# One store where there were two and four: expert outputs, query and key weights, and the final sum in a two-layer YOCO step

## The chip, the cores and the metric

The kernel runs on one core of one Trainium2 chip. The metric is device time in microseconds (us) of one execution, from start to end; lower is better. TensorE, VectorE, ScalarE, GpSimd and SyncE are called PE, DVE, ACT, POOL and SP in the profile. 16 DMA engines move the data; the queues that SP, ACT and POOL fill are q1, q10 and q0 there.

## What is computed

One inference step of a two-layer decoder trunk in float32, width 1024, for 512 prompt tokens and 32 sample tokens (8 sequences of 4). Layer 0 is an HGRN2 recurrence, layer 1 is differential attention over shared keys and values, which for the sample tokens reach back over 2048 cached positions in pages. Behind each stands a mixture of 16 experts, of which each token uses two:

```python
def hier_moe(h, w_group, w_sub, w_gate, w_up, w_down):
    ...
    eid = gidx[..., None] * MOE_EPG + idx                      # two experts of one group
    gates = jnp.einsum('btke,btk->bte', jax.nn.one_hot(eid, MOE_EXPERTS, dtype=F32), w2)
    hid = jax.nn.silu(jnp.einsum('btd,edf->btef', h, w_gate)) * jnp.einsum('btd,edf->btef', h, w_up)
    hid = hid * gates.astype(h.dtype)[..., None]
    return jnp.einsum('btef,efd->btd', hid, w_down)            # D = 1024, f = 256

for l in range(DEPTH):                                         # DEPTH = 2
    h = h + mixer(rmsnorm(h, norm_mix_w[l]))                   # HGRN2, then differential attention
    h = h + hier_moe(rmsnorm(h, norm_ffn_w[l]), ...)
    if l == 0:                                                 # keys and values of layer 1
        kv = rmsnorm(h, kv_norm_w) @ w_kv
y = rmsnorm(h, final_norm_w)
```

The queries of layer 1 are `rmsnorm(h, norm_mix_w[1]) @ b_w_q`.

## The kernel before

The 544 tokens stand as five tiles: four of 128 prompt rows (t = 0 to 3) and one of 32 sample rows (t = 4). The residual stream `h` stays in SBUF. The work is one program with blocks for the stages; in a block each engine runs its own list of instructions in the order in which the code writes them, and semaphores tie the engines together. Nothing reorders them, so a change of order in the code is a change of order on the engine.

**The expert loop** (class Experts, from line 1519), the same for both layers. A token's row has been sent to a slot of its expert in DRAM (`slots_x`); an expert has 96 slots (CAP), 64 wide and 32 narrow. SP loads each expert's 96 rows, its gate and up weights (two loads of 1 MB) and its down weights (1 MB) into a ring of five experts' slots, all in one queue. For expert e PE computes gate and up (L1739, L1744), turns the rows of expert e + 1 (L1716), computes down for expert e - 1 (L1764, L1768) and turns the hidden rows of e (L1752, L1753). ACT takes the SiLU (L1613, L1614), DVE multiplies with the up half (L1662) and moves the turned hidden rows out (L1669, L1671). The 64 wide rows of the result stand in bank 5 as 128 partitions x 512: columns 0 to 511 of the rows on partitions 0 to 63, columns 512 to 1023 on partitions 64 to 127. The 32 narrow rows stand in bank 6 as four such quarters of 256 columns. ACT copies the wide ones to SBUF (`YW`, L1620), DVE the narrow ones (`YN`, L1678). ACT then issues the stores to `slots_y` in DRAM: two DMAs for the wide rows (L1623) and four for the narrow ones (L1597), one for each half or quarter; each adds 16 to `y_out` of that buffer when it has landed, and `STORES` = 6 is what the waits reckon with. The narrow rows of the last expert are stored by SP. `slots_y` has a row of 1024 floats for each slot.

If more tokens want an expert than it has slots, a branch behind the loop takes the rest (`more > 0`). Each engine reads the number of these blocks from SBUF (`more_blocks`, L1549) and jumps over the branch where it is zero.

**Behind the loop.** `finish` (L1790) runs on PE: it waits until all stores have landed, then adds to `finished`. POOL waits for that and issues ten indirect gathers, two for each token tile (a token's two experts), from `slots_y`.

- Layer 0: the gathers are those of L1811, the sample tile first (`SAMPLE_FIRST`). DVE adds them, times the gates, to `h` (L1824); `add(dve, i)` adds both rows of the i-th tile of that order. Then the norm for layer 1 is made tile by tile: squares on ACT (L2177), root (L2179), scaling on DVE (L2190), turned on PE (L2205), and copied into `xT` by DVE and ACT (L2218, `out_first`; L2225, `out_second`). PE's sample queries (L412) follow on the sample tile.
- Class Projections prepares the query and key weights meanwhile. Each of the four halves (q0, q1, k0, k1, 128 x 4096) is multiplied with the norm's weight row. ACT does q0 and k0 with eight activations each (L2272, x16 in the profile), DVE q1 and k1 with one instruction each of 128 x 4096 (L2281). The table `PROJECT_SCALED` holds which unit of PE's projections waits for how many of these. A few loads of pages and of weights for this stage stand in SP's queue behind the last experts'.
- Layer 1 (class SumOnBanks, from L1864; `last_block`, L1945): the sum is made on the banks. PE enters `h` of a tile by a multiplication with the identity (`residual`, L1904, two matmuls per tile), then adds the gathered rows with diagonal matrices of the gates (`add`, L1913). Tile t uses banks 2t and 2t + 1. Tiles 0 and 1 are entered before PE's `finish`, tiles 2 and 3 behind it, all of them behind the branch. ACT squares the banks (L1924), DVE scales them with the final norm (L1941), SP stores the result.

**At the start** ACT issues twelve small loads (class Setup, L199 to L203): six of 8 rows x 128 (L199, weight vectors of 1024) and six of a single row (L200, L201, L203: two norm weights and four lambda vectors).

## Time and profile before

| | |
|---|---|
| three runs | 1472.49, 1474.75, 1483.41 us, median 1474.75 us |
| the profiled execution | 1480.49 us, its span 1478.7 us |
| mean granted TensorE clock | 0.935 |
| PE busy | 1305.8 us, 88% of the span |
| DVE busy | 723.8 us, 49% |
| ACT busy | 411.2 us, 28% |
| POOL busy | 176.3 us, 12% |
| moved by DMA | 348.15 MB in 133,902 packets |
| expert loop of layer 0 | about 487 to 657 us |
| expert loop of layer 1 | about 1274 to 1441 us |

All times are microseconds from the start of the span in that one execution. A row of the timeline has start, duration, engine, line of the kernel, operation, output<-input by the program's names, shapes, count, and in brackets how long the engine sat idle before it and what ended that. "ACTq" and "SPq" are the sequencers that issue DMAs. PE counts a float32 matmul as several passes, so 8 matmuls stand as x16. The granted clock is a share of full speed. A share of DMA is the mean busy share of the 16 engines.

### The profile page before, as it was taken

The page shows a single profiled execution, that of the slowest core. Times are in us where ns is not written, and L with a number is a line of the kernel's source. Part 1 is how long each engine was busy: PE and PEld are TensorE (multiplying, and loading weights), DVE is VectorE, ACT ScalarE, POOL GpSimd, SP SyncE. Part 2 cuts the span into 40 slices and gives each one's busy share as a digit, 9 for nine tenths or more (in the row PEclk, how much of TensorE's full clock was granted, in tenths as well). Part 3 has the DMA queues.
Part 4 walks back from the last instruction along what each step waited for, and adds up shares of the span by engine and source line. Part 5 has one row for each costly group of instructions (what it writes and reads, how often), then busy time and mean ns, then how long its engine had stood idle before and what let it go on. Part 6 is the DMA issues. An engine that isn't in the chain of part 4 may idle for free. (4 is left out here: it accounts for less than half of the span.)

```text
span 1478.7 us, 29953 instructions
## 1 busy us (share of the span) xinstructions
PE 1305.8 (88%) x11855; PEld 770.3 (52%) x11855; DVE 723.8 (49%) x1881; ACT 411.2 (28%) x1098; POOL 176.3 (12%) x247
## 2 busy tenths in 40 slices
PE   6999999998799998976999989868778699899897
PEld 3445565565356654534555545445454355755543
DVE  4435777676655311137343544377874465411123
ACT  3024445453210211133213121134455211121112
POOL 2002223322011000013021100100100001000002
PEclk9999999999898899997999999988988799799998
DMA  6150435223804899994465899799999631899935
GB/s 231 58 149 6 134 107 182 74 77 131 288 36 170 308 367 356 320 329 169 150 220 218 329 347 361 302 405 374 408 378 343 219 140 52 339 379 343 338 94 189
DMA packets 133902, 348.15 MB, mean 235 GB/s; under 512 B 22603, under 2 KB 52478, under 8 KB 125566
## 3 DMA queue, kind: packets, MB, share of 16 engines
q1 hardware_dynamic: 115378, 311.53, 59.0%
q10 hardware_dynamic: 13388, 16.82, 3.4%
q0 software_dynamic: 4992, 17.83, 3.3%
q8 instruction: 97, 1.59, 0.4%
q14 instruction: 47, 0.39, 0.1%
HBM read 302.61 MB, written 43.52 MB: 234 GB/s over the span
## 5 line engine op out<-in xcount | busy, mean ns | idle before, releaser
L409 PE MATMUL bank<-wring,xT 128*128 128x512 f32 x448 | 200.4, 602 | 0.0
L409 PEld LDWEIGHTS bank<-wring,xT 128*128 128x128 f32 x448 | 84.1, 192 | 100.6 <-issue 100.5
L1440 PE MATMUL bank<-wring,xT 128*128 128x512 f32 x256 | 120.2, 623 | 2.0 <-DVE xT L1360 2.0
L883 PE MATMUL bank<-xT,wring 128*128 128x512 f32 x256 | 113.7, 602 | 3.9 <-DVE hgrn_g L707 3.9
L2803 DVE STREAM_TRANSPOSE attn_k_pages<-attn_k_pages 128x1024 f32<-128x1024 f32 x64 | 77.6, 1232 | 40.4 <-DMA attn_k_pages<-cache_k 39.9
L883 PEld LDWEIGHTS bank<-xT,wring 128*128 128x128 f32 x256 | 48.7, 192 | 65.3 <-issue 59.8
L1440 PEld LDWEIGHTS bank<-wring,xT 128*128 128x128 f32 x256 | 49.6, 200 | 60.1 <-issue 59.9
L2803 DVE STREAM_TRANSPOSE wring<-wring 128x1024 f32<-128x1024 f32 x44 | 52.5, 1222 | 49.2 <-DMA wring<-cache_k 49.2
L785 DVE COPY_PREDICATED gla_att<-level_masks,bank 128x512 f32<-128x512 int32 x48 | 35.1, 731 | 72.1 <-PE bank L903 72.0
L2316 PE MATMUL bank<-xT,wring 128*128 128x512 f32 x128 | 56.9, 597 | 0.0
L903 PE MATMUL bank<-gla_qe,gla_ke 128*128 128x128 f32 x384 | 49.9, 285 | 0.0
L1662 DVE TENSOR_TENSOR hgrn_g<-hgrn_g,bank 128x128 f32<-128x128 f32 x32 | 7.8, 284 | 84.7 <-ACT hgrn_g L1613 84.7
L1662 DVE TENSOR_TENSOR attn_qo<-attn_qo,bank 128x128 f32<-128x128 f32 x32 | 7.8, 284 | 82.6 <-ACT attn_qo L1613 82.6
L903 PEld LDWEIGHTS bank<-gla_qe,gla_ke 128*128 128x128 f32 x384 | 46.4, 197 | 3.1 <-DVE gla_att L785 2.6
L569 ACT ACTIVATE gla_diff<-gla_diff 128x512 f32<-128x512 f32 (+1 forms) x48 | 30.6, 638 | 57.5 <-DVE gla_diff L750 48.4
L1620 ACT ACTIVATE moe_norm_w<-bank 128x512 f32<-128x512 f32 x32 | 19.1, 597 | 81.5 <-PE bank L1768 81.5
L2926 ACT ACTIVATE attn_shared<-attn_shared,pa_stat 128x128 f32<-128x128 f32 (+2 forms) x64 | 35.2, 556 | 17.3 <-DVE pa_stat L2786 17.3
L844 POOL TENSOR_TENSOR gla_ke<-gla_k,gla_diff 128x256 f32<-128x256 f32 x40 | 32.1, 802 | 53.3 <-ACT gla_diff L569 53.3
L2610 POOL TENSOR_SCALAR attn_shared<-attn_shared 128x512 f32<-128x512 f32 x8 | 11.9, 1491 | 222.4 <-DVE pa_stat L2786 144.3
L2316 PEld LDWEIGHTS bank<-xT,wring 128*128 128x128 f32 x128 | 23.7, 190 | 27.8 <-issue 27.8
L2680 PE MATMUL bank<-attn_k_pages,sa_q 128*32 128x128 f32 x1024 | 31.1, 273 | 7.4 <-DVE sa_red L2812 7.4
L840 POOL TENSOR_TENSOR gla_ke<-gla_k,gla_diff 128x544 f32<-128x544 f32 x8 | 10.9, 1362 | 212.5 <-ACT gla_diff L562 212.5
(460 smaller groups left out, 2403.2 us busy)
## 6 DMA issues: line engine op xcount, KB each, us to landing
attn_k_pages<-cache_k SPq DMA_DIRECT2D x64, 512.0 KB, 7.6
wring<-cache_v SPq DMA_DIRECT2D x56, 512.0 KB, 7.8
wring<-cache_k SPq DMA_DIRECT2D x44, 512.0 KB, 7.0
moe_wd<-moe_w_down SPq DMA_DIRECT2D x20, 1024.0 KB, 13.6
attn_shared<-cache_v SPq DMA_DIRECT2D x40, 512.0 KB, 5.7
wring<-moe_w_gate SPq DMA_DIRECT2D x18, 1024.0 KB, 11.2
wring<-moe_w_up SPq DMA_DIRECT2D x18, 1024.0 KB, 14.8
wring<-a_w_in SPq DMA_DIRECT2D x16, 1024.0 KB, 10.5
```

Source lines behind the costliest of these rows:

```text
L409: last = nc.tensor.matmul(bank[:, :], xT[:, c, cols(t)], w[:, c, :], start=(c == 0), stop=(c == DC - 1))
L569: nc.scalar.activation(diff[i % 2][:, 0:w], diff[i % 2][:, 0:w], ACT.Exp).then_inc(exp_ready, 1)
L785: nc.vector.copy_predicated(A[:, :, :], bcast(k.levelmask[:, i, :].bitcast(I32), 1, [P, PT, P]), k.ps[3 + i % 2][:, :].rearrange("p (c n) ...
L844: nc.gpsimd.tensor_tensor(blocks(KE[j][:, :], size)[:, :, lo], blocks(kk[:, 0:SEQ], size)[:, :, lo], blocks(diff[j % 2][:, 0:SEQ], size)[: ...
L883: last = nc.tensor.matmul(bank[:, :], lhsT, k.xT[:, c, 0:SEQ], start=(c == 0), stop=(c == DC - 1))
L903: last = nc.tensor.matmul(k.ps[3 + i % 2][:, part], KE[i][:, part], QE[i][:, part], start=True, stop=True)
L1440: last = nc.tensor.matmul(bank[:, :], k.xT[:, c, cols(t)], w[:, c, :], start=(c == 0), stop=(c == DC - 1))
L1620: nc.scalar.activation(self.YW[u][:, :], k.ps[5][:, :], ACT.Copy).then_inc(self.y_a, 1)
L2316: last = nc.tensor.matmul(bank[:, :], w[:, c, (t % 4) * P:(t % 4 + 1) * P], k.xT[:, c, 0:SEQ], start=(c == 0), stop=(c == DC - 1))
L2680: last = nc.tensor.matmul(out.rearrange("p (r x) -> p r x", r=GROUP), Q[b % 2][:, h, i, :], keys.K[s][:, :, at:at + QUAD], start=(i == 0), ...
L2803: nc.vector.transpose(page, page).then_inc(keys_turned, 1)
L2926: last = nc.scalar.activation(part, part, ACT.Exp, bias=s[:, x, 2 + c:3 + c], accum_out=s[:, x, 4 + c:5 + c])
```

## The change

1. **Two stores for each expert in place of six.** The wide rows go out in one DMA, the narrow ones in one. The destination is written as [2, 64 rows, 512 columns] and [4, 32 rows, 256 columns], the source is the whole tile of 128 partitions. `STORES` becomes 2.
2. **Scaling of weights on DVE.** `gates_ready` becomes a general hook `beside`, called behind the hidden rows of the last two experts. In layer 0 it now runs `weights_by_vector(0)` (k1 whole) behind expert 14's and `weights_by_vector(1)` (the first half of q1) behind expert 15's; the second half of q1 follows behind the branch.
3. **Scaling on ACT.** q0 whole as before; then the root of the first tile, the first half of k0, the copies of the first tile, the second half of k0, the root of the second tile. `PROJECT_SCALED` and the wait of the sample queries follow suit.
4. **Adds of the second tile on DVE** are split: the first choice before `out_first(0)`, the second behind it.
5. **The end of layer 1.** Tiles use banks (0, 1), (4, 5), (6, 7), (2, 3). PE enters three tiles ahead of the branch: tile 0 behind the last down matmuls, tile 1 when ACT has copied bank 5, tile 2 when DVE has copied bank 6. Inside the branch they are closed first and entered again at its end. Tile 3 follows behind the branch. `finish` is run by DVE there instead of PE; in layer 0 it stays on PE. Inside the branch DVE waits for the stores.

```diff
@@ Experts
-NB, STORES = 2, 6
+NB, STORES = 2, 2
         eng.wait_ge(self.y_v, j + 1)
-        for n in range(4):
-            eng.dma_start(self.slot_rows(row, WIDE, NARROW)[:, n * 2 * P:(n + 1) * 2 * P], self.YN[u][n * NARROW:(n + 1) * NARROW, :])\
-                .then_inc(self.y_out[u], 16)
+        eng.dma_start(self.slot_rows(row, WIDE, NARROW).rearrange("r (n c) -> n r c", n=4), self.YN[u][:, :])\
+            .then_inc(self.y_out[u], 16)
...
-            for n in range(2):
-                act.dma_start(self.slot_rows(row, 0, WIDE)[:, n * HB:(n + 1) * HB], self.YW[u][n * WIDE:(n + 1) * WIDE, :])\
-                    .then_inc(y_out[u], 16)
+            act.dma_start(self.slot_rows(row, 0, WIDE).rearrange("r (n c) -> n r c", n=2), self.YW[u][:, :])\
+                .then_inc(y_out[u], 16)
...
-            if e >= E - 2 and gates_ready is not None:
-                gates_ready(dve, e - (E - 2))
+            if e >= E - 2 and beside is not None:
+                beside(dve, e - (E - 2))
...
+            if last_layer:
+                dve.wait_ge(self.y_out[0], 16 * STORES * (loads_before(NB, 0) + MORE))
...
         pe.wait_ge(routing.blocks_ready, 1)
+        if on_free_banks is not None:
+            on_free_banks(0)
+            pe.wait_ge(self.y_a, E)
+            on_free_banks(1)
+            pe.wait_ge(self.y_v, E)
+            on_free_banks(2)
         more = self.more_blocks(pe)
         with pe.If(more > 0):
+            if on_free_banks is not None:
+                for t in range(3):
+                    on_free_banks(t, start=False, stop=True)
...
+            if on_free_banks is not None:
+                for t in range(3):
+                    on_free_banks(t)
@@ SumOnBanks, last_block
     def banks(self, t):
-        return [self.k.ps[2 * (t % PT) + i] for i in range(2)]
+        first = (0, 4, 6, 2)[t % PT]
+        return [self.k.ps[first + i] for i in range(2)]
...
-            ffn.experts.vector(dve, total.diagonal)
+            ffn.experts.vector(dve, total.diagonal, True)
+            ffn.experts.finish(dve)
...
-            ffn.experts.tensor(pe)
             pe.wait_ge(ffn.mix.added, 2 * NT)
-            for t in range(2):
-                total.residual(pe, t)
-            ffn.experts.finish(pe)
-            for t in range(2, PT):
-                total.residual(pe, t)
+            ffn.experts.tensor(pe, lambda t, **flags: total.residual(pe, t, **flags))
+            total.residual(pe, 3)
@@ Projections
-        for landed, kind, row in ((k.weights_landed(self.first + 1), "q", 1), ((self.k1_in, 32), "k", 2)):
-            dve.wait_ge(*landed)
-            tile = self.W[kind, 1][:, :, :]
+        landed, kind, row, c = (((self.k1_in, 32), "k", 2, slice(0, DC)),
+                                (k.weights_landed(self.first + 1), "q", 1, slice(0, DC // 2)),
+                                (k.weights_landed(self.first + 1), "q", 1, slice(DC // 2, DC)))[n]
+        dve.wait_ge(*landed)
+        tile = self.W[kind, 1][:, c, :]
...
-        pe.wait_ge((self.scaled_a, self.scaled_v)[i], 1)
+        pe.wait_ge(*((self.scaled_a, 1), (self.scaled_v, 3))[i])
...
-        self.weights_by_vector(dve)
+        self.weights_by_vector(dve, 2)
         add(dve, 0)
         turn_page(0, 0)
         norm.scale(dve, ch, 0)
-        add(dve, 1)
+        add(dve, 1, (0,))
         norm.out_first(dve, 0)
+        add(dve, 1, (1,))
...
-        self.weights_by_act(act)
+        queries_0, keys_0, half = (0, "q", 1), (2, "k", 2), DC // 2
+        self.weights_by_act(act, queries_0, range(DC))
         norm.load_table(act)
         norm.root(act, 0)
+        self.weights_by_act(act, keys_0, range(half))
         norm.out_second(act, 0)
+        self.weights_by_act(act, keys_0, range(half, DC))
         norm.root(act, 1)
-PROJECT_SCALED = {0: ("act", 2), 1: ("dve", 2), 14: ("pool", 1), V_SAMPLE: ("pool", 2)}
+PROJECT_SCALED = {0: ("act", 3), 1: ("dve", 1), 14: ("pool", 1), V_SAMPLE: ("pool", 2)}
...
-                ffn.vector(dve)
+                ffn.vector(dve, proj.weights_by_vector)
```

ACT, the stores of expert 0 of layer 0 and what stands ahead of them, before. `moe_norm_w` holds the wide rows, `hgrn_g` the narrow ones (and what L1606 and L1614 write), `slots_y` is in DRAM:

```order
L1613 ACTIVATE hgrn_g<-bank 128x128
L1614 ACTIVATE hgrn_g<-bank 128x128
L1606 ACTIVATE hgrn_g<-bank 128x384
L1620 ACTIVATE moe_norm_w<-bank 128x512
L1623 DMA slots_y<-moe_norm_w 64x512 x2
L1597 DMA slots_y<-hgrn_g 32x256 x4
```

And now:

```order
L1612 ACTIVATE hgrn_g<-bank 128x128
L1613 ACTIVATE hgrn_g<-bank 128x128
L1605 ACTIVATE hgrn_g<-bank 128x384
L1619 ACTIVATE moe_norm_w<-bank 128x512
L1621 DMA slots_y<-moe_norm_w 2x64x512
L1596 DMA slots_y<-hgrn_g 4x32x256
```

Six DMAs have become two, with an outer count of 2 and of 4; the activations are the same.

DVE, before, from the end of layer 0's loop (behind the branch) on; `wring` holds q1 and `attn_shared` k1:

```order
L2876 MEMSET sa_lam_row 128x4
L2877 COPY sa_lam_row<-row_gains 128x4
L2281 TENSOR_TENSOR wring<-wring,column_weights 128x4096
L2281 TENSOR_TENSOR attn_shared<-attn_shared,column_weights 128x4096
L1824 SCALAR_TENSOR_TENSOR h<-hgrn_v,stat,h 32x1024
L1824 SCALAR_TENSOR_TENSOR h<-hgrn_g,stat,h 32x1024
```

DVE now, from the hidden rows of expert 14 to the branch:

```order
L1669 TENSOR_REDUCE hgrn_g<-bank 128x2x32
L2293 TENSOR_TENSOR attn_shared<-attn_shared,column_weights 128x4096
L1660 TENSOR_TENSOR hgrn_g<-hgrn_g,bank 128x128 x2
L1676 COPY hgrn_g<-bank 128x256
L1667 COPY hgrn_g<-bank 128x2x64
L1669 TENSOR_REDUCE hgrn_g<-bank 128x2x32
L2293 TENSOR_TENSOR wring<-wring,column_weights 128x2048
L1676 COPY hgrn_g<-bank 128x256
L1549 TENSOR_LOAD slots_and_blocks
```

The keys' scaling stands before the multiplications of expert 15 (L1660), half of the queries' before the last copy of narrow rows (L1676); the other half stays behind the branch, ahead of the adds.

PE, the end of layer 1's loop, before, without the branch's own rows:

```order
L1764 MATMUL bank<-moe_wd,attn_qo 64x512 x4
L1768 MATMUL bank<-moe_wd,attn_qo 32x256 x8
L1549 TENSOR_LOAD slots_and_blocks
L1549 ISA x2
L1782 COMPARE_AND_BRANCH
...
L1782 UNCONDITIONAL_BRANCH
L1904 MATMUL bank<-h,ident 128x512 x8
L1913 MATMUL bank<-attn_qo,wring 128x512 x10
```

And now:

```order
L1764 MATMUL bank<-moe_wd,attn_qo 64x512 x4
L1768 MATMUL bank<-moe_wd,attn_qo 32x256 x8
L1917 MATMUL bank<-h,ident 128x512 x6
L1549 TENSOR_LOAD slots_and_blocks
L1549 ISA x2
L1788 COMPARE_AND_BRANCH
...
L1788 UNCONDITIONAL_BRANCH
L1917 MATMUL bank<-h,ident 128x512 x2
L1926 MATMUL bank<-attn_qo,wring 128x512 x10
```

Six of the eight residual matmuls have moved ahead of the read of the number of blocks and the jump.

## Rows read from the trace of the kernel before

**Rows 1.** The page's head.

```profile
span 1478.7 us, 29953 instructions
```

**Rows 2.** Windows in both loops: us, busy of L1620 (count), clock, DMA share, GB/s.

```profile
500.00:619.60 119.60, 6.57 (x11) 0.97 1.02 354
1280.00:1392.60 112.60, 5.97 (x10) 0.98 1.00 348
```

**Rows 3.** PE's timeline, the last wait for gathered rows in each loop.

```profile
619.62 0.88 PE L1716 MATMUL bank<-ident,hgrn_g 96*128 96x96 f32 x8 [2.14 <-DMA hgrn_g<-slots_x]
...
1392.65 0.88 PE L1716 MATMUL bank<-ident,attn_qo 96*128 96x96 f32 x8 [1.90 <-DMA attn_qo<-slots_x]
```

**Rows 4.** ACT's queue from 1436 to 1441, the last two experts' stores.

```profile
1436.16 1.12 ACTq L1623 DMA_DIRECT2D slots_y<-moe_norm_w  x2
1437.33 2.02 ACTq L1597 DMA_DIRECT2D slots_y<-attn_qo  x4
...
1440.10 1.42 ACTq L1623 DMA_DIRECT2D slots_y<-moe_norm_w  x2
```

**Rows 5.** DMA from 0 to 14: packets and share; an issue, KB each.

```profile
q10 hardware_dynamic: 108, 0.03, 0.9%
...
hgrn_g<-norm_mix_w ACTq DMA_DIRECT2D x2, 4.0 KB
```

**Rows 6.** DMA from 520 to 540: packets, MB and share; an issue with landing.

```profile
q1 hardware_dynamic: 1253, 6.38, 90.9%
q10 hardware_dynamic: 704, 0.79, 11.3%
...
slots_y<-moe_norm_w ACTq DMA_DIRECT2D x4, 128.0 KB, 6.9
```

**Rows 7.** DMA from 1438 to 1438.5, then an issue from 1440 to 1440.5.

```profile
q10 hardware_dynamic: 58, 0.11, 96.9%
...
slots_y<-moe_norm_w ACTq DMA_DIRECT2D x1, 128.0 KB, 2.3
```

**Rows 8.** Timeline at the end of layer 0's loop.

```profile
648.67 0.49 DVE L1662 TENSOR_TENSOR hgrn_g<-hgrn_g,bank 128x128 f32<-128x128 f32 x2 [5.34 <-ACT hgrn_g L1613]
...
655.18 0.42 DVE L1678 COPY hgrn_g<-bank 128x256 f32<-128x256 f32 x1 [3.12 <-PE bank L1768]
...
656.65 4.42 DVE L2281 TENSOR_TENSOR wring<-wring,column_weights 128x4096 f32<-128x4096 f32 x1
658.47 9.91 ACT L2272 ACTIVATE wring<-wring,column_weights 128x512 f32<-128x512 f32 x16 [2.56 <-issue]
659.71 2.12 POOL L1811 DMA_INDIRECT hgrn_v<-slots_y,slots_and_blocks  x1 [173.64 <-PEq L1795]
...
660.99 4.42 DVE L2281 TENSOR_TENSOR attn_shared<-attn_shared,column_weights 128x4096 f32<-128x4096 f32 x1
662.14 4.01 POOL L1811 DMA_INDIRECT hgrn_g<-slots_y,slots_and_blocks  x1 [0.30 <-issue]
...
670.71 1.27 DVE L1824 SCALAR_TENSOR_TENSOR h<-hgrn_v,stat,h 32x1024 f32<-32x1024 f32 x1 [5.30 <-DMA hgrn_g<-slots_y,slots_and_blocks]
...
679.33 0.28 ACT L2225 ACTIVATE xT<-bank 128x128 f32<-128x128 f32 x1 [4.43 <-PE bank L2205]
...
680.94 6.76 PE L412 MATMUL bank<-wring,xT 128*32 128x128 f32 x192 [1.65 <-DVE xT L2218]
```

**Rows 9.** Timeline at the end of layer 1's loop; last, a gather's landing.

```profile
1439.92 2.54 SPq L1597 DMA_DIRECT2D slots_y<-attn_qo  x4
...
1442.62 9.93 PE L1904 MATMUL bank<-h,ident 128*128 128x512 f32 x16 [3.22 <-issue]
...
1443.93 0.99 POOL L1887 DMA_INDIRECT attn_qo<-slots_y,slots_and_blocks  x1 [170.79 <-PEq L1795]
...
1452.38 8.75 PE L1913 MATMUL bank<-attn_qo,wring 128*128 128x512 f32 x20
...
attn_qo<-slots_y,slots_and_blocks POOLq DMA_INDIRECT x1, 4.2
```

More of the change, by code:

```diff
@@ L1813, in gpsimd, with add @@
                     .then_inc(self.landed[i], 16)
-    def add(self, dve, i):
+    def add(self, dve, i, choices=range(TOPK)):
         k, t = self.k, SAMPLE_FIRST[i]
         dve.wait_ge(self.landed[i], 16 * TOPK)
-        for j in range(TOPK):
+        for j in choices:
             n = TOPK * i + j
@@ L1848, in scalar, with vector @@
         self.experts.scalar(act)
-    def vector(self, dve):
+    def vector(self, dve, beside=None):
         self.mix.vector(dve)
-        self.experts.vector(dve)
+        self.experts.vector(dve, beside)
     def tensor(self, pe):
@@ L1898, in diagonal, with residual @@
         last.then_inc(self.diagonals, 1)
-    def residual(self, pe, t):
+    def residual(self, pe, t, start=True, stop=False):
         k = self.k
@@ L1904, in residual @@
             self.nc.tensor.matmul(bank[0:rows(t), :], k.ident[0:rows(t), 0:rows(t)], k.h[0:rows(t), t, i * HB:(i + 1) * HB],
[L1905 removed]
+                                  start=start, stop=stop)
     def add(self, pe, t):
@@ L2263, in first_pages_in, with weights_by_act, weights_by_vector @@
             self.keys.load_k(sp, 0, r)
-    def weights_by_act(self, act):
+    def weights_by_act(self, act, which, chunks):
         k = self.k
-        for n, kind, row in ((0, "q", 1), (2, "k", 2)):
-            act.wait_ge(*k.weights_landed(self.first + n))
-            for c in range(DC):
-                part = self.W[kind, 0][:, c, :]
-                last = self.nc.scalar.activation(part, part, ACT.Copy, scale=k.cw[:, row, c:c + 1])
-            last.then_inc(self.scaled_a, 1)
-    def weights_by_vector(self, dve):
-        k = self.k
-        for landed, kind, row in ((k.weights_landed(self.first + 1), "q", 1), ((self.k1_in, 32), "k", 2)):
-            dve.wait_ge(*landed)
-            tile = self.W[kind, 1][:, :, :]
-            self.nc.vector.tensor_tensor(tile, tile, bcast(k.cw[:, row, :], 2, [P, DC, HB]), ALU.mult).then_inc(self.scaled_v, 1)
+        n, kind, row = which
+        act.wait_ge(*k.weights_landed(self.first + n))
+        for c in chunks:
+            part = self.W[kind, 0][:, c, :]
+            last = self.nc.scalar.activation(part, part, ACT.Copy, scale=k.cw[:, row, c:c + 1])
+        last.then_inc(self.scaled_a, 1)
+    def weights_by_vector(self, dve, n):
+        k = self.k
+        landed, kind, row, c = (((self.k1_in, 32), "k", 2, slice(0, DC)),
[3 more added lines that the diff above has]
+        tile = self.W[kind, 1][:, c, :]
+        self.nc.vector.tensor_tensor(tile, tile, bcast(k.cw[:, row, c], 2, [P, c.stop - c.start, HB]), ALU.mult).then_inc(self.scaled_v, 1)
     def value_weights_by_pool(self, pool, i):
```

13 lines of the change are left out of this document (6 added, 7 removed).

## The prediction

> **What bounds the kernel now.** I read the windows over the two expert loops first, then what TensorE waits for in them, then what the stores cost the DMA engines, and last the timelines at the two places where a loop ends. The span is 1478.7 us [rows 1] in a run of 1480.49 us, so 1.8 us lie around it; the median of the three runs shown is 1474.75, 5.7 below that run, and I carry differences over to the median unchanged.
>
> The reader is to see that the DMA engines are full in both expert loops: share 1.02 from 500 to 619.6 and 1.00 from 1280 to 1392.6, with 11 and 10 experts' stores in these stretches [rows 2]. TensorE is just ahead of them. It waits for the gathered rows of the next expert, 2.14 us at 619.62 and 1.90 us at 1392.65 [rows 3], each time the last such wait of its loop: up to there an expert takes as long as its loads, and behind it as long as its matmuls. A loop then ends in a chain: last copy out, stores, `finished`, the gathers by POOL, the adds. So three things can change the time: work given to the DMA engines inside the loops, the time at which the last store lands, and what stands between the gathers and the next matmul.
>
> **The stores.** Before, an expert's rows leave in six DMAs of 64 or 32 rows, issued in 1.12 and 2.02 us [rows 4]. Now there are two: one writes [2, 64 rows, 512], one [4, 32 rows, 256], from 128 partitions each. Bytes and data packets stay the same: the row of two experts says 704 packets [rows 6], and 2 x (128 + 128 data + 6 x 16) = 704, so a DMA of 64 or of 32 rows ended with a small packet on each of 16 engines. What is open is over how many engines the new ones go. The trace has a case with few rows at the start: six loads of 8 rows and six of one row are all that the queue carried, and it moved 108 packets [rows 5] (the code's lines 199 to 203 give the counts). Data are 6 x 8 + 6 x 1 = 54, so 54 small ones are left, and 6 x 8 + 6 x 1 is again 54 (with 16 each they would be 192). A load of 8 rows ran on 8 engines, one of one row on one: the outermost count sets the number of engines when it is small. Here the outermost count of the destination is 2 and 4, that of the source 128. No row shows a DMA with unlike counts. I take the smaller, since a share of the work must be a whole part of both sides: 2 engines for the wide store, 4 for the narrow one.
>
> The Trainium skill, DMA: Bandwidth & Descriptors, section "Why a DMA increments its semaphore by 16 and not by 1", says it outright: the number of engines is the largest up to 16 that divides the slowest dimension of both access patterns, so an outer dimension of 2 confines the DMA to two. The 108 and 704 packets above agree with it; by it the sum is the one below, and by a split along the source's 128 rows it would be that of the first rival.
>
> The price: the stores of two experts took 11.3% of 16 engines x 20 us = 36.2 us [rows 6], 18.1 us for one expert, or 1.13 us on each engine. Two thirds of the bytes are wide: 12.1 us, on two engines 6.0 each. The narrow 6.0 us on four are 1.5 each. If the four include the two, which I assume, as both would begin at the same end, the busiest engines carry 7.5 us in place of 1.13: +6.4 per expert (5.0 if they don't share). From above: in a quiet half microsecond 58 packets of mostly 2 KB took 96.9% of 8 us [rows 7], 0.134 us each; 64 of them are 8.6, with the narrow 1.5 that makes 10.1, +9.0. I take 6.4, since the row that it comes from lies in the full stretch where it counts.
>
> Each load of weights or rows is split evenly over 16 engines and has landed when the fullest one is done. So in the full stretches every expert's loads land 6.4 us later per store put ahead of them: 11 x 6.4 = **70 us** in layer 0 and 10 x 6.4 = **64 us** in layer 1 [rows 2]. At +9.0 it is 99 and 90, at 5.0 it is 55 and 50. ScalarE is freed of some 2 us of issuing per expert, which hides behind matmuls anyway.
>
> **Where the loops end.** Layer 1: the last two wide stores are issued at 1436.16 and 1440.10 [rows 4]. At 8.6 + 1.5 us each on the busiest engines they are worked off at 1446.3 and 1456.4, and with the 1.2 us that a store needs beyond its packets (it landed in 2.3 us, 8 x 0.134 of it moving [rows 7]) the last lands at 1457.6; the first gather began at 1443.93, so it is 13.7 late. A gather landed after 4.2 us [rows 9]: the first add can start at 1461.8, not 1452.38, +9.4. The three residual tiles are done by then, so nothing is won by moving them; and after the long wait the first adds run at the low clock, as the residuals did before: the residuals' 16 passes took 9.93 us, while the adds' took 8.75 / 20 = 0.44 each, so 2.9 us were lost to the clock [rows 9]. Together **+12 us**. That VectorE now signals in TensorE's place costs nothing against a store that lands at 1457.6: even a branch as long as TensorE's 3.22 us [rows 9] is over by 1443.2.
>
> Layer 0: the last stores are late in the same way, and loads of pages and weights stand on the same engines: **+14 us** at least. Against it stand the scalings. VectorE's two took 4.42 us each, and POOL's first two gathers took 2.12 and 4.01 us under them [rows 8], where a gather of layer 1 takes 0.99 [rows 9]; the first add began at 670.71 [rows 8]. Now the key weights go into the idle 5.34 us before 648.67 (4.42 fit, with 0.9 to spare) and half the query weights into the 3.12 us before 655.18 (2.2 fit) [rows 8]. The last 2.2 us run from 656.65 to 658.9, ahead of the gathers. The two gathers then take 2.3 us (2 x 0.99 and 0.3 between) instead of the 6.4 from 659.71 to 666.15: -4.2. One add of 1.27 us is no longer ahead of the copy that frees TensorE at 680.94: -1.3. ScalarE's first key half, 4 x 0.62 us (9.91 / 16), fits into its idle 4.43 us before 679.33; the second makes the next square 1.4 us later, which the 6.76 us of matmuls at 680.94 cover [rows 8]. If the query weights land late on the full engines, VectorE's copy of the last expert waits behind them, a few us. Sum **-5.5 us**; net for this end +8.5.
>
> **Sum.** 70 + 8.5 + 64 + 12 = 154.5 us: 1480.5 becomes 1635, and the median 1474.75 becomes **1629 us**.
>
> **Rivals.** (1) The stores keep 16 engines, because the split follows the source's 128 rows. For it speaks only that no row shows unlike counts. Then the loops lose nothing and save 64 small packets per expert, at the mean of 0.051 us (36.2 / 704) 0.2 us per expert, at most 4. `finished` comes about 1.4 us sooner at each end, as four SP stores of 2.54 us become one [rows 9]; layer 0 gains 5.5 + 1.4. In layer 1 the six moved matmuls are 12 passes, which run while TensorE would have idled 3.22 us for the branch, if its sequencer works on the branch while matmuls are queued. Then residuals end near 1446.5, the first gather lands near 1447, and the adds gain about 5; if it doesn't, the idle time and the low clock only move behind them: 0. Take 4. Together -11, with some of the packets -13: 1462 us (1458 to 1468). This is the one that ends on the other side, and the number of engines decides it: already at 8 for both stores the busiest carry 18.1 / 8 = 2.3 us, +1.1 per expert or 24 us in all, more than everything else gains.
>
> (2) Few engines, but the loads don't wait for them: if the full share is a limit of the memory and not of each engine, the two could do more while the rest idle. Against it: the share of all engines is 1.0, and the load queue and the stores add up to it (90.9% and 11.3% [rows 6]). Then only the ends count: 14 + 12 - 5.5 = +20.5, 1495 us.
>
> (3) The upper price: each 2 KB packet takes 0.134 us in the full stretches too. 99 + 90 + 20.5 = +209, 1684 us.
>
> **Chances.** Few engines with loads held up 0.77 (of it 0.12 near rival 3), rival 2 0.06, 16 engines 0.17. The likeliest gives 1629; its own range, by 5.0 and 9.0 per expert, is 1595 to 1684, and 1560 to 1700 with what I don't know of the waits between. The range that leaves out rival 1 alone and the tails is 1490 to 1700. A measurement can tell about 1% (15 us) from no change. Rival 1 lies at -0.9% and is faster by over 1% one time in four: faster 0.05, same 0.12, slower 0.83.
>
> **What would show it.** Right: packets of the ACT queue per expert fall from 352 to 262 (256 data, 2 + 4 small) and not to 288; a wide store takes 10 us and more to land instead of 2.3 in the quiet stretch; TensorE waits about 5 us before every transposed expert from the sixth or so on, for slots_x; the mean share of the 16 DMA engines in the loops falls to about 0.65; the first two gathers of layer 0 take about 1 us each. Wrong: 288 small-and-data packets, shares still at 1.0, loops as long as before. If the waits are there but shorter than 5 us, the price per packet is off; if the loops stay and only the ends move, rival 2 holds.

## The result, and the profile after

The changed kernel takes 1584.96 us (median of 4 runs, 1580.79 to 1589.07) against 1479.08 us for the kernel before in the same rounds: 1.0716 times as long, 95% interval 1.0678 to 1.0754, 106 us more. The profiled execution has a span of 1579.0 us, 100.3 more than before [rows 1]. The forecast was 1629 us and slower: the sign and the number of engines held, the size (+154.5 us) was half as large again as what was measured, and one step of the way to it, who waits, was wrong.

First the ACT queue on the page of the changed kernel (packets, MB, share of 16 engines):

```profile
span 1579.0 us, 29827 instructions
q10 hardware_dynamic: 10628, 16.81, 2.9%
```

Before it was 13,388 packets, so 2,760 went. ACT issues 32 wide and 30 narrow merged stores in the two loops. At a small packet for each engine used, the old form has 32 x 32 + 30 x 64 = 2,944 of them, and 2 and 4 engines give 32 x 2 + 30 x 4 = 184: the difference is 2,760, to the packet. Two engines for the wide store and four for the narrow one is thus what the trace of the changed kernel shows. The Trainium skill says the same (DMA: Bandwidth & Descriptors, "Why a DMA increments its semaphore by 16 and not by 1"): the number of engines is the largest up to 16 that divides the slowest dimension of both sides, here of 2 and 128, and of 4 and 128.

The windows of the loops answer to [rows 2] (us, busy time of ACT's copy and their count, granted clock, DMA share, GB/s):

```profile
500.00:619.60 119.60, 4.78 (x8) 0.84 0.73 265
487.00:660.00 173.00, 6.57 (x11) 0.87 0.72 261
```

In the stretch in which 11 experts' rows went out before, 8 do now, and the DMA engines as a whole are busy for 0.73 of it, where it was 1.02. The timeline shows who waits (ACT, DVE and PE around expert 3 of layer 0; `ACTq` issues DMAs):

```profile
514.54 0.55 ACTq L1621 DMA_DIRECT2D slots_y<-moe_norm_w  x1
...
515.13 15.57 ACTq L1596 DMA_DIRECT2D slots_y<-hgrn_g  x1
...
522.31 1.07 PE L1768 MATMUL bank<-moe_wd,hgrn_g 128*32 128x256 f32 x16
...
530.79 0.28 ACT L1612 ACTIVATE hgrn_g<-bank 128x128 f32<-128x128 f32 x1 [16.28 <-issue]
...
531.17 0.48 DVE L1660 TENSOR_TENSOR hgrn_g<-hgrn_g,bank 128x128 f32<-128x128 f32 x2 [15.53 <-ACT hgrn_g L1612]
...
531.71 0.48 PE L1752 MATMUL bank<-ident,hgrn_g 128*128 128x128 f32 x1 [8.33 <-DVE hgrn_g L1660]
532.38 6.35 PE L1739 MATMUL bank<-wring,hgrn_g 128*64 128x256 f32 x32
```

ACT stands 15.57 us in the issue of the narrow store, behind the wide one of the same expert. Its SiLU (L1612) comes late by that, DVE's product (L1660) behind it, and PE's turn of the hidden rows (L1752) 8.33 us after its matmuls have ended; the gate matmuls that follow run at the lower clock (6.35 us at a granted clock of 0.57, so mostly 1.2 GHz, where the same matmuls took 3.67 at 1.00, 2.4 GHz, from 514.14 on). The wait that the forecast named, for `slots_x` ahead of L1716, is gone. By its line, before (us in total, matmuls and weight loads counted alike, times):

```profile
  DMA hgrn_g<-slots_x: 19.3, 11
  DMA attn_qo<-slots_x: 14.8, 11
```

and in the changed kernel:

```profile
  issue: 5.8, 29
  DMA attn_qo<-slots_x: 0.3, 1
```

and the wait of L1752 on the page of the changed kernel, one row for each layer, nearly all of it new (before, 0.3 us stood under that releaser in each layer):

```profile
L1752 PE MATMUL bank<-ident,hgrn_g 128*128 128x128 f32 x16 | 6.1, 383 | 49.5 <-DVE hgrn_g L1660 49.4
...
L1752 PE MATMUL bank<-ident,attn_qo 128*128 128x128 f32 x16 | 5.8, 365 | 39.0 <-DVE attn_qo L1660 38.9
```

Together 88.3 us, most of what the loops lose.

At the end of layer 1 no loads are left, and the two engines can be seen alone (DMA from 1540 to 1545 us):

```profile
q10 hardware_dynamic: 114, 0.23, 12.0%
```

12.0% of 16 engines are 1.9 engines, and 114 packets of 2 KB took 0.12 x 16 x 5 = 9.6 us, 0.084 us each. With both queues at work on them, while the other engines are idle (699 to 703 us), the queues' packets go out in equal numbers:

```profile
q1 hardware_dynamic: 42, 0.15, 9.3%
q10 hardware_dynamic: 41, 0.06, 4.0%
```

The two engines together moved 0.21 MB in these 4 us, 26 GB/s each.

To see where the 100.3 us lie I read the same marks in the timeline of every run. L0 and L1 are the loops, from the first gate matmul (L1739) to ACT's last copy of wide rows, each mark at its start; then come the first gather by POOL, the first add, the sample queries (L412 on PE), the middle (projections and attention) and, behind L1, the first gather, PE's first add on the banks and the end. All in us:

| kernel | L0 | to gather | to add | to queries | middle | L1 | to gather | to add | to end |
|---|---|---|---|---|---|---|---|---|---|
| before | 167.8 | 4.4 | 11.0 | 10.2 | 593.6 | 164.9 | 4.5 | 8.5 | 26.3 |
| changed | 228.3 | 13.2 | 7.4 | 7.8 | 585.2 | 205.2 | 13.4 | 4.3 | 28.7 |
| two_stores_alone | 228.7 | 13.2 | 7.4 | 9.0 | 585.1 | 207.6 | 13.5 | 4.5 | 28.6 |
| wide_merged | 210.1 | 15.9 | 7.0 | 9.0 | 593.2 | 197.0 | 11.6 | 4.5 | 28.5 |
| narrow_merged | 169.8 | 7.4 | 6.9 | 9.0 | 584.2 | 168.2 | 6.1 | 4.7 | 28.1 |
| six_stores | 170.0 | 4.9 | 7.1 | 9.0 | 589.8 | 168.0 | 6.3 | 4.5 | 28.1 |
| outer_16 | 166.3 | 4.1 | 6.9 | 9.0 | 584.1 | 171.3 | 4.3 | 4.5 | 27.1 |
| outer_8 | 173.0 | 8.1 | 6.8 | 9.0 | 586.9 | 169.5 | 6.1 | 4.6 | 28.4 |
| outer_4 | 188.3 | 15.6 | 7.8 | 7.7 | 588.6 | 187.5 | 9.6 | 4.6 | 29.1 |
| light_down | 205.8 | 13.2 | 7.1 | 9.0 | 597.1 | 183.3 | 13.5 | 4.3 | 29.3 |
| pool_issues | 179.1 | 10.5 | 7.0 | 9.0 | 585.0 | 175.2 | 11.7 | 4.4 | 28.9 |
| pool_waits | 166.8 | 4.7 | 7.2 | 9.0 | 586.0 | 172.6 | 6.4 | 4.3 | 28.1 |
| entry_alone | 171.0 | 4.6 | 7.2 | 9.0 | 585.4 | 168.3 | 4.7 | 7.3 | 26.3 |
| tail_alone | 174.1 | 4.6 | 10.2 | 10.2 | 585.1 | 167.3 | 6.1 | 4.4 | 27.5 |

The loops take 60.5 + 40.3 = 100.8 us more. The end of layer 0 takes +8.8 - 3.6 - 2.4 = +2.8, that of layer 1 +8.9 - 4.2 + 2.4 = +7.1. The stretch ahead of the first mark is 2.1 us shorter, and the middle 8.4 shorter: together 100.2 (the marks are rounded). The middle is no effect of the change: in tail_alone its program is the one before, and it took 585.1 us there. It is 584 to 597 us over the fourteen runs of the table, with no order by the edits. Each trace has 16 copies of wide rows in each layer, so the branch for extra blocks ran in none.

two_stores_alone, which has none of the edits at the two ends, shows what they are worth in the changed kernel. Its first add also comes 7.4 us after the first gather, and in layer 1 its three stages are 13.5, 4.5 and 28.6 us. The stores keep the gathers waiting for so long that VectorE has finished its scalings by then, and TensorE its residuals, with or without the edits. At the two ends only 1.2 us, 7.8 against 9.0 up to the sample queries, can be the edits' own.

### The profile page after: what moved, and what is told of

It is laid out like the page before. It is cut to its first block and busy times, and to the rows that moved or that the text cites. A ratio compares the mean times of both kernels' runs of the same rounds, so it can differ in the third digit from the quotient of the medians.

```text
span 1579.0 us, 29827 instructions
## 1 busy us (share of the span) xinstructions
PE 1321.3 (84%) x11855; PEld 785.3 (50%) x11855; DVE 721.6 (46%) x1882; ACT 409.6 (26%) x1098; POOL 171.5 (11%) x247
## 5 line engine op out<-in xcount | busy, mean ns | idle before, releaser
L883 PEld LDWEIGHTS bank<-xT,wring 128*128 128x128 f32 x256 | 48.1, 190 | 64.2 <-issue 58.7
L1660 DVE TENSOR_TENSOR hgrn_g<-hgrn_g,bank 128x128 f32<-128x128 f32 x32 | 7.8, 284 | 146.2 <-ACT hgrn_g L1612 146.2
L1660 DVE TENSOR_TENSOR attn_qo<-attn_qo,bank 128x128 f32<-128x128 f32 x32 | 7.8, 284 | 126.6 <-ACT attn_qo L1612 126.6
L1752 PE MATMUL bank<-ident,hgrn_g 128*128 128x128 f32 x16 | 6.1, 383 | 49.5 <-DVE hgrn_g L1660 49.4
L1739 PE MATMUL bank<-wring,hgrn_g 128*64 128x256 f32 x288 | 43.7, 470 | 0.5 <-DVE hgrn_g L1654 0.5
L1612 ACT ACTIVATE hgrn_g<-bank 128x128 f32<-128x128 f32 x16 | 4.4, 277 | 150.3 <-issue 121.1
L1739 PE MATMUL bank<-wring,attn_qo 128*64 128x256 f32 x288 | 39.3, 434 | 0.5 <-DVE attn_qo L1654 0.5
L1752 PE MATMUL bank<-ident,attn_qo 128*128 128x128 f32 x16 | 5.8, 365 | 39.0 <-DVE attn_qo L1660 38.9
```

The lines of the kernel that those rows point to most:

```text
L883: last = nc.tensor.matmul(bank[:, :], lhsT, k.xT[:, c, 0:SEQ], start=(c == 0), stop=(c == DC - 1))
L1739: nc.tensor.matmul(out, self.XT[u][:, c, 0:WIDE], moe.WGU[s][:, :, c, n * P:(n + 1) * P], start=(c == 0), stop=(c == DC - 1))
```

## The experiments

Twelve kernels; each ratio is to the kernel before, timed beside it, with its 95% interval.

### The six stores put back: six_stores

```diff
-NB, STORES = 2, 2
+NB, STORES = 2, 6
-            act.dma_start(self.slot_rows(row, 0, WIDE).rearrange("r (n c) -> n r c", n=2), self.YW[u][:, :])\
-                .then_inc(y_out[u], 16)
+            for n in range(2):
+                act.dma_start(self.slot_rows(row, 0, WIDE)[:, n * HB:(n + 1) * HB], self.YW[u][n * WIDE:(n + 1) * WIDE, :])\
+                    .then_inc(y_out[u], 16)
```

and the narrow rows in four DMAs in the same way.

> The changed kernel with the six stores of before; the other edits stay. Theory F (few engines: the whole loss is the two wide and four narrow engines of the merged stores): both loops are as long as before (about 168 and 165 us from the first gate matmul to the last copy), the wait of TensorE ahead of L1752 is gone and the one for slots_x is back; the other edits win what the first rival counted without its fewer stores, 5.5 us in layer 0 and 0 to 5 in layer 1: 1465 to 1475 us, ratio to before 0.990 to 0.997. Theory R (part of the loss comes from the scalings inside the loop or from the end on VectorE): the time stays above 1485.

Measured: 1473.76 us, ratio 0.9963 (0.9933 to 0.9994). The loops are back at 170.0 and 168.0 us. The whole loss was in the stores; what else the change does is worth 1 to 10 us where the stores are not in its way. The waits are those of the kernel before again, as expected: 0.3 us in each layer ahead of the turn of the hidden rows, and 19.4 and 18.3 us for `slots_x`, counted as above.

### The stores alone: two_stores_alone

The reverse: the kernel before, with the two merged stores and `STORES` = 2 as its only edit.

> The kernel before with only the merged stores. Theory F: the whole loss and a little more, as the gains of the other edits are missing: 1585 to 1600 us, ratio 1.07 to 1.085. Theory R: clearly less than the changed kernel, under 1560.

Measured: 1588.61 us, ratio 1.0776 (1.072 to 1.0832), loops 228.7 and 207.6. As theory F had it. That is 3.7 us above the changed kernel, which the intervals don't tell from nothing.

### One of the two merged: wide_merged, narrow_merged

```diff
-NB, STORES = 2, 2
+NB, STORES = 2, 5          # wide_merged: narrow rows in four DMAs
+NB, STORES = 2, 3          # narrow_merged: wide rows in two DMAs
```

> The changed kernel, wide rows in one DMA of [2, 64, 512], narrow ones in four DMAs as before. Theory F: the fullest engine carries for each expert 0.221 MB of loads, 0.131 of wide rows and 0.008 of narrow ones, 0.360 in place of 0.385 MB: at the 14.4 us of an expert in the changed kernel that is 13.5 (if the two wide engines were among the narrow four) or still 14.4 (if not): ratio 1.05 to 1.075. Rival M (each merged DMA costs alike, because it is merged, whatever its outer count): about half of the loss, ratio 1.03 to 1.04.

> The changed kernel, narrow rows in one DMA of [4, 32, 256], wide ones in two DMAs as before. Theory F: the fullest engine carries 0.221 + 0.016 + 0.033 = 0.270 MB for each expert where it was 0.246: at most 0.5 us more per expert, 0 to 16 us in all, less what the other edits win: ratio 0.99 to 1.01. Rival M: about half of the loss, ratio 1.03 to 1.04.

Measured: wide_merged 1566.93 us, ratio 1.061 (1.0557 to 1.0664); narrow_merged 1473.78 us, ratio 0.9984 (0.9954 to 1.0013). Of two merged DMAs, one with an outer count of 2 and twice the bytes, the other with 4, the first costs nearly everything, the second nothing that can be measured: rival M falls. On top of the wide store the narrow one does cost something: 228.3 - 210.1 = 18.2 us in layer 0, 1.1 per expert, and 205.2 - 197.0 = 8.2 in layer 1, 0.5 per expert. That speaks for it that the four engines include the two, as the forecast assumed; so does the window from 699 to 703 us, where q10's 41 packets are of 1.5 KB in the mean, so of both stores, and only 13.3% of 16 engines, 2.1, are at work.

### The outer count as the only thing changed: outer_16, outer_8, outer_4

Here both stores stay one DMA each, with the same source and the same bytes, and the destination's half and quarter rows are walked in another order, so that the outer count is 16, 8 or 4:

```diff
-            act.dma_start(self.slot_rows(row, 0, WIDE).rearrange("r (n c) -> n r c", n=2), self.YW[u][:, :])\
+            act.dma_start(self.slot_rows(row, 0, WIDE).rearrange("(m a) (n c) -> (a n) m c", n=2, a=8), self.YW[u][:, :])\
```

with a = 8, 4 and 2 for the wide rows, and n = 4 with a = 4, 2 and 1 for the narrow ones. A single DMA that leaves every row in its place and still uses 16 engines was not tried.

> The changed kernel with both stores still one DMA each, from the same 128 partitions and with the same bytes, but written in another order of the half and quarter rows: [16, 8, 512] and [16, 8, 256]. The rows of a token then hold parts of other slots' rows, so layer 0's mixture output and what follows from it differ. Theory F: 16 engines for both; the loops are as with six stores, packets of the ACT queue 144 + 144 for an expert, ratio 0.985 to 1.00. Rival M (one merged DMA of three dimensions is slow in itself): ratio 1.06 to 1.08 as in the changed kernel.

> As the one before with [8, 16, 512] and [8, 16, 256] (contents moved in the same manner). Theory F: the fullest engine carries 0.221 MB of loads and 0.049 of stores for an expert, the 0.270 MB of the kernel with the narrow rows merged, which cost nothing: ratio 0.99 to 1.005. The forecast's own price (+1.1 us per expert already at 8 engines, 24 us in all) would give 1.005 to 1.015. Rival M: 1.06 to 1.08.

> As the two before with [4, 32, 512] and the narrow store of the changed kernel [4, 32, 256] (contents of the wide rows moved). Theory F: 0.221 + 0.066 + 0.033 = 0.320 MB on the fullest engine, between 0.270 (no loss) and 0.360 (2.8 us per expert with the wide rows merged): about 1.5 us per expert, 25 to 50 us in all, ratio 1.015 to 1.035. Rival M: 1.06 to 1.08.

Measured: 1472.35 us, ratio 0.9961 (0.9927 to 0.9995); 1482.41, ratio 1.0038 (1.0012 to 1.0064); 1525.58, ratio 1.0331 (1.0285 to 1.0378). With the changed kernel at 2 and 4 (1.0716) the time rises with one quantity, the bytes on the fullest engine:

| outer counts | MB on the fullest engine, per expert | loops L0, L1 | ACT's longest issue of a narrow store | ratio |
|---|---|---|---|---|
| 16, 16 | 0.246 | 166.3, 171.3 | 0.69 | 0.9961 |
| 8, 8 | 0.270 | 173.0, 169.5 | 0.62 | 1.0038 |
| 4, 4 | 0.320 | 188.3, 187.5 | 5.66 | 1.0331 |
| 2, 4 | 0.385 | 228.3, 205.2 | 16.20 | 1.0716 |

The ACT queue carried 11,436, 10,940 and 10,692 packets: with 62 stores at 16, 8 and 4 small ones each, 992, 496 and 248 over 10,444, again to the packet. The last column but one is from the answers by the line of the narrow store (min/median/max ns of one issue), here in the changed kernel:

```profile
L1596 ACTq DMA_DIRECT2D slots_y<-hgrn_g x15: 632/8862/16196, 505.7 to 708.4; - x15
```

with an outer count of 4:

```profile
L1596 ACTq DMA_DIRECT2D slots_y<-hgrn_g x15: 547/602/5660, 509.4 to 673.3; - x15
```

and of 16:

```profile
L1596 ACTq DMA_DIRECT2D slots_y<-hgrn_g x15: 607/612/692, 506.9 to 650.3; - x15
```

An issue that is not held takes about 0.6 us in all of them; what is above that is waiting, and for the narrow stores it appears only where few engines carry them.

### Who issues: pool_issues

All merged stores moved to POOL, which has nothing to do in the loops:

```diff
+    def gpsimd(self, pool):
+        for e in range(EXPERTS):
+            u = e % NB
+            pool.wait_ge(self.y_a, e + 1)
+            pool.dma_start(self.slot_rows(e * CAP, 0, WIDE).rearrange("r (n c) -> n r c", n=2), self.YW[u][:, :])\
+                .then_inc(self.y_out[u], 16)
+            self.store_narrow(pool, e, u, e * CAP)
```

ACT keeps its copies and drops its stores, SP drops that of the last narrow rows.

> The changed kernel with all merged stores issued by POOL, which is idle in the loops, so that ACT is never held while it issues. Theory T (throughput: the two engines that carry 0.385 MB for each expert are the limit, and ACT's long issue is only where the wait shows): the wait moves to ACT's copy, which needs the buffer of two experts before, or to the loads; the loops stay as long, ratio 1.055 to 1.08. Theory A (the loss arises because ACT stands in the issue while its SiLU is due): the loops recover most of it, ratio under 1.03. If POOL's queue spreads a store over other engines than ACT's does, the time falls too, and then the landing of a wide store, not the issue, shows it.

Measured: 1499.14 us, ratio 1.0127 (1.0069 to 1.0185), loops 179.1 and 175.2. This doesn't tell theories T and A apart, because the third case of the expectation came true. DMA from 520 to 540 us:

```profile
DMA  9997998999999899999999999899999999898999
...
q1 hardware_dynamic: 1123, 6.09, 90.0%
q0 software_dynamic: 1157, 0.71, 13.0%
...
slots_y<-moe_norm_w POOLq DMA_DIRECT2D x2, 256.0 KB, 13.2
slots_y<-hgrn_g POOLq DMA_DIRECT2D x2, 128.0 KB, 21.8
```

All engines are full again, with nearly the loads' share of before (90.0% against 90.9% [rows 6]): POOL's queue spreads the same access pattern over all engines. Over the whole run q0 carried 1,024 more packets of 4 bytes than in the changed kernel, 16 for each of the 64 stores, and the rows as 3,072 packets of 4 KB. It pays with landings of 13.2 and 21.8 us, where it was 6.9 and 7.6 before, and with a first gather 6 to 7 us later at both ends. ACT's copy now waits for the stores of two experts before, 66.6 us in layer 0 and 54.8 in layer 1, and the loops stay 10 to 11 us longer than in the kernel before. The Trainium skill (DMA: Bandwidth & Descriptors, the section named above) has both kinds of queue follow the same rule, but notes that POOL's queue gives some direct copies all 16 engines on this chip; this trace agrees, with 16 end packets for each store.

### Fewer bytes of loads beside the same stores: light_down

```diff
-                moe.load_down(sp, (e - 1) % NW, e - 1 + NW)
+                moe.load_down(sp, (e - 1) % NW, e - 1 + NW, P)   # only 128 of the 1024 columns
```

> The changed kernel, but of the down weights of experts 5 to 15 only the first 128 of 1024 columns are loaded (the rest are those of an earlier expert, so the mixtures' outputs differ). The stores are untouched: two and four engines. The fullest engine then carries 0.221 - 0.057 = 0.164 MB of loads and 0.164 of stores for an expert, 0.328 MB, about what it carried with an outer count of 4 (0.320), where the loops took 188 us each. Theory T (the work on the fullest engine sets the pace, whoever is seen waiting): both loops come down to 185 to 200 us from 228 and 205, ratio to before 1.02 to 1.045. Theory A (ACT is held by the wide store as such: 64 packets on each of two engines, each in turn with a load's packet): the loops keep their length, ratio 1.06 to 1.075.

Measured: 1549.06 us, ratio 1.0461 (1.0428 to 1.0494), loops 205.8 and 183.3. Theory A, by which the loops keep their length, falls: 22 us went from each without a change to a store. Theory T's range for the whole (up to 1.045) is missed by a little. In layer 1 the loop is 2 us below theory T's range and 4 shorter than that of outer_4, which carries nearly the same bytes on its fullest engine (0.320 against 0.328 MB); in layer 0 it is 6 us above that range and 17.5 above outer_4. The issue of the narrow store still took up to 12.6 us:

```profile
L1596 ACTq DMA_DIRECT2D slots_y<-hgrn_g x15: 558/5792/12597, 509.1 to 682.0; - x15
```

Most of the 17.5 us lie at the end of that loop, in what the 0.328 MB leave out. The last three gaps between ACT's copies of wide rows are 10.2, 14.1 and 14.1 us, 38.4 together, where those of outer_4 are 9.5, 8.7 and 5.3, 23.5 together. From 655 to 695 us SP's queue moves the loads for the next stage:

```profile
q1 hardware_dynamic: 3266, 7.42, 53.7%
q10 hardware_dynamic: 790, 1.17, 7.9%
```

That is 0.46 MB of loads on each engine, and on the two that carry the wide stores 0.49 of three experts' rows besides: 0.95 MB in 40 us, 24 GB/s. So the work on the fullest engine, with all loads counted, explains most of the length in both layers. Whether holding ACT costs anything beyond that work was not separated.

### The other edits apart: entry_alone, tail_alone, pool_waits

entry_alone is the kernel before with the edits on the weights' scaling and on the adds of layer 0; tail_alone is the kernel before with those at the end of layer 1. pool_waits is six_stores with this in SumOnBanks, and without VectorE's `finish`:

```diff
-        pool.wait_ge(self.ffn.experts.finished, 1)
+        pool.wait_ge(experts.routing.blocks_ready, 1)
+        more = experts.more_blocks(pool)
+        with pool.If(more > 0):
+            pool.wait_ge(experts.y_out[0], 16 * STORES * (loads_before(NB, 0) + MORE))
+        for u in range(NB):
+            pool.wait_ge(experts.y_out[u], 16 * STORES * loads_before(NB, u))
```

> The kernel before with only the edits on the weights' scaling and on the order around layer 0's adds. From the stages of the run with six stores: gather to first add 7.1 us where it was 11.0, first add to sample queries 9.0 where it was 10.2, so 4 to 5 us less: ratio 0.995 to 0.999. Rival: DVE's scaling in the loop holds up a copy there and takes it back: 1.000.

> The kernel before with only the edits at the end of layer 1 (three residual tiles ahead of the branch, other banks, VectorE signals). From the stages of the run with six stores: the last copy to the end takes 38.9 us where it took 39.2, since the residuals come 5 us earlier but the first gather comes 1.8 us later and the adds run at the lower clock: ratio 0.998 to 1.002. The forecast's rival had -4 us here: 0.997.

> The changed kernel with six stores, and in layer 1 POOL waits itself for the landed stores (it reads the number of extra blocks during the loop) instead of a signal from VectorE. With six stores the first gather began 3.8 us after the end of the last store's issue, against 1.5 in the kernel before, where TensorE signals. If VectorE's branch makes the signal late, the first gather comes about 2.3 us sooner, the wait of TensorE ahead of the first add (2.91 us) nearly goes, the adds stay nearer the high clock: 3 to 5 us less than six stores, ratio 0.990 to 0.996. If the stores' landing sets it, nothing changes.

Measured: entry_alone 1473.92 us, ratio 0.9958 (0.993 to 0.9987); tail_alone 1479.2 us, ratio 1.0004 (0.9973 to 1.0034); pool_waits 1472.01 us, ratio 0.9956 (0.9926 to 0.9985), not to be told from six_stores.

The edits at the entry are what wins, and they do so where the stores land early: the first add comes 7.2 us after the first gather where it came 11.0 after, the sample queries 9.0 after it where it was 10.2. Their rows in six_stores:

```profile
655.80 2.28 DVE L2295 TENSOR_TENSOR wring<-wring,column_weights 128x2048 f32<-128x2048 f32 x1
...
658.99 0.42 DVE L1678 COPY hgrn_g<-bank 128x256 f32<-128x256 f32 x1 [0.91 <-PE bank L1770]
...
664.07 0.88 POOL L1825 DMA_INDIRECT hgrn_v<-slots_y,slots_and_blocks  x1 [176.40 <-PEq L1809]
...
665.26 0.87 POOL L1825 DMA_INDIRECT hgrn_g<-slots_y,slots_and_blocks  x1 [0.30 <-issue]
...
671.20 1.27 DVE L1838 SCALAR_TENSOR_TENSOR h<-hgrn_v,stat,h 32x1024 f32<-32x1024 f32 x1 [8.45 <-DMA hgrn_g<-slots_y,slots_and_blocks]
```

The scaling stands in DVE's idle time with 0.91 us to spare ahead of the copy, and the first two gathers take 0.88 and 0.87 us, where they took 2.12 and 4.01 beside DVE's large multiplications [rows 8].

The end of layer 1 gives back what it wins, here in pool_waits:

```profile
1434.83 7.41 PE L1923 MATMUL bank<-h,ident 128*128 128x512 f32 x16
...
1441.33 0.99 POOL L1906 DMA_INDIRECT attn_qo<-slots_y,slots_and_blocks  x1 [180.43 <-DMA slots_y<-attn_qo]
...
1445.60 9.61 PE L1932 MATMUL bank<-attn_qo,wring 128*128 128x512 f32 x18 [3.37 <-DMA attn_qo<-slots_y,slots_and_blocks]
```

The residuals now follow on the last matmuls at the high clock, 7.41 us for 16 passes at a granted clock of 1.00 (2.4 GHz), where they took 9.93 at 0.71 [rows 9]. Then TensorE idles 3.37 us, and it is the adds that start at the lower clock: 9.61 us for 18 passes, 0.53 each at 0.83, which is partly 1.2 GHz, where they took 0.44 at 1.00. POOL's own wait ends with the stores' landing, so no signalling engine is at fault for the gather; pool_waits' hope for an earlier one falls. That the first gather comes 6.1 to 6.4 us behind the last copy in tail_alone, six_stores and pool_waits, but 4.5 and 4.7 in the kernel before and in entry_alone, is a cost of this tail. In all three, the last three increments of the semaphore that counts the stores come 1.1 to 1.7 us behind the rest, and a 16 KB packet of queue q8, which the profile calls instruction, starts 2.8 us behind the copy, while the last stores are on their way. In the kernel before and in entry_alone such a packet starts 0.6 us behind the copy, and the increments come without a gap. That the packet holds one engine up is likely, but was not tested. (In outer_16, which has the same tail and one store where there are four, the gather comes after 4.3 us.)

Both entry_alone and six_stores are faster than the changed kernel, and by 0.4% than the kernel before, with intervals that end just below 1.

## Why the prediction came out as it did

- **The number of engines: right.** "2 engines for the wide store, 4 for the narrow one", and that the four include the two. Shown by the packet counts and by the runs with other outer counts. Rival 1, 16 engines, fell. What it described is outer_16: -5.4 us by the medians (-11 to -1 by the interval), where it had -11 to -13. The profiled run has the end of layer 0 at 20.0 us, 5.6 shorter than before, where the rival had 6.9, and that of layer 1 at 35.9, 3.4 shorter, where it had 4.
- **The price for an expert, +6.4 us: the term that was mis-sized.** From the gate matmuls of the fifth expert to those of the last, an expert took 14.40 us in layer 0 of the changed kernel (532.38 to 690.78 us, eleven experts) and 10.63 before (525.82 to 642.74): +3.8. In layer 1 it was 13.50 against 10.47: +3.0. The forecast took the 0.139 MB that the fullest engine carries more at the rate of the full stretch, 22 GB/s (6.38 MB in 0.909 x 320 = 291 us [rows 6]), and added them to the pace of then. By that rate 0.246 MB are 11.2 us and 0.385 MB are 17.5. But the two engines work faster when the others idle: the load packets of the stretch from 699 to 703 us moved 0.15 MB in 0.093 x 16 x 4 = 6.0 us, 25 GB/s, and with both queues an engine moved 26 GB/s. 0.385 MB at 26 GB/s are 14.8 us, 3.6 more than 11.2. There was no time to spare on the engines before (share 1.02 [rows 2]); what the forecast left out is that load packets take less time when the other engines idle: 4 KB took 0.159 us in that stretch, and 0.197 in the mean of the window before [rows 2]. 2 KB of a store took about the same in both, 0.084 and 0.087; the 0.094 of the forecast (12.1 us for 128) has some of the narrow and end packets in it. Rival 2 had that idea, for the whole effect; rival 3's 0.134 us for 2 KB was not seen in the full stretches.
- **The number of experts charged: too small, and luckily so.** The forecast charged 11 and 10 experts by the windows of [rows 2]; the loops lose 60.5 and 40.3 us, 3.8 and 2.5 over all 16. In layer 0 the eleven experts above account for 41.5 of the 60.5, 8.7 arise before them and 10.3 behind. The stall began with the fourth expert, though in the kernel before the first five gaps between copies were 9.5 us, as short as those at the end of the loop. In layer 1 it began as early, 7.0 us and then 33.4, but the loads of the last experts end before the loop does, the last issues take 0.56 us again, and nothing is lost there. A price too high and a count too small made 70 and 64 us; without the second error the sum would have been farther off.
- **The range.** By its own terms its lower end, at 5.0 per expert, is 55 + 50 + 20.5 = 125.5 us above 1474.75, so 1600 us and not 1595. The measured 1585 us lies below it, and inside the stated 1560 to 1700 only by the allowance for "what I don't know of the waits between".
- **Who waits: wrong.** "TensorE waits about 5 us before every transposed expert from the sixth or so on, for slots_x" was to be seen; that wait vanished. The ACT sequencer is held in the issue of the narrow store, and through SiLU it holds everything; the loads, whose ring is five experts deep, get time they did not have. The forecast had booked ACT's issuing as a saving of 2 us. The work on the two engines sets the pace all the same (light_down), which is why the sum was of the right kind.
- **The ends: right in kind, too large.** First gather +13.7 us late in layer 1: measured +8.9, as a wide store takes 64 x 0.084 = 5.4 us on its two engines and not 8.6. The quiet half microsecond of [rows 7], in which 58 packets took 0.134 us each, was one with all engines writing at once; it was no upper price for two. +12 us became +7.1. In layer 0 +14 became +8.8. Of the -5.5 us of the other edits -3.6 and -2.4 stand in the table, but two_stores_alone has -3.6 and -1.2 without them. The forecast counted as a gain that the gathers would no longer run beside VectorE's scalings, and had itself put the gathers 14 us later, behind the scalings in any case. The edits' own part is 1.2 us. That moving the residuals wins nothing, as the forecast said, is so. "A branch as long as TensorE's ... is over by 1443.2" was not at issue: the stores landed later.
- **DMA share 0.65 in the loops, packets 262 per expert, first gathers of about 1 us:** 0.73 in the window of [rows 2], 0.69 and 0.64 over the whole loops; 262 for the experts whose narrow rows ACT stores; 0.89 and 0.87 us. For "10 us and more to land" no view gives a landing of a merged wide store; the first gathers, which wait for the last of them, start 13.2 and 13.4 us behind the last copy.
- **At 8 engines "24 us in all":** 1482.4 us against 1472.4 with 16, so 10.

## What to carry to other kernels

Merging DMAs on ACT's queue by making the pieces the outermost dimension took the transfer off all but as many engines as there were pieces: fewer instructions and packets, the same bytes, and an engine that carries four to eight times its share of the stores. Before such an edit, work out the bytes on the fullest engine beside what the loads already put there; 10% more (0.270 MB against 0.246) cost 10 us of 1475 in one kernel (outer_8) and nothing measurable in another (narrow_merged), 57% more cost 106. Take the rate for the sum from a stretch in which as few engines work as will do so after the edit: here they moved 26 GB/s each and not 22. And look for the cost not only at whoever waits for the data: the sequencer that issues the next DMA can be held, with all compute queued behind it.

## What was not expected of the hardware

- The issue of a narrow store on ACT's queue, 0.6 us when nothing holds it, took up to 16.2 us behind a wide store on two engines, and up to 5.7 behind one on four. With 8 or 16 it never exceeded 0.7.
- POOL's queue ran the [2, 64, 512] store over all 16 engines (16 end packets for each store), for landings of 13.2 us and more.
- Two queues with work on the same two engines got equal numbers of packets through: 42 and 41 in 4 us.
- An engine moved 26 GB/s while the other fourteen idled, and 22 when all were full.
